# Two of each block's eight left-hand one-hots on GpSimd, in the gate stage of a hybrid Hyena/GLA/PEER layer

## What is computed

```python
best, pos = lax.top_k(cand_s, PEER_TOPK)
idx = jnp.take_along_axis(cand_i, pos, axis=-1)
gate = jax.nn.softmax(best, axis=-1)
...
a = jax.nn.gelu(jnp.einsum('td,tkd->tk', xt, u_tab[it]))
return jnp.einsum('tk,tkd->td', gt * a, v_tab[it])
```

## Time and profile before

| | |
|---|---|
| median of 3 runs | 2192.99 us (2191.74, 2192.99, 2200.29) |
| profiled execution, its own time | 2182.85 us |
| its span | 2181.1 us |
| TensorE busy | 2045.7 us, 94% of the span |
| VectorE busy | 1522.5 us, 70% |
| ScalarE busy | 822.2 us, 38% |
| GpSimd busy | 688.2 us, 32% |
| gate stage, first to last left-hand one-hot | 925.7 to 1403.5 us |
| granted TensorE clock, mean of the span | 0.97 of full speed |

### The profile page before, as it was taken

The page is one execution under the profiler, slowest core; times in us unless marked ns, Lnnn a source line. Parts: engine busy times, 40 slices in busy tenths (PEclk is TensorE's granted clock), DMA queues, the critical chain, the costliest instruction groups (busy, mean ns, idle before and its releaser), DMA issues.

```text
span 2181.1 us, 28455 instructions
## 1 busy us (share of the span) xinstructions
PE 2045.7 (94%) x9877; PEld 1631.1 (75%) x9877; DVE 1522.5 (70%) x3164; ACT 822.2 (38%) x1507; POOL 688.2 (32%) x469
## 2 busy tenths in 40 slices
PE   7999999797998999898888899979999999999998
PEld 3554454645998999887777788878888888888886
DVE  4221415623789999898888888748887687877876
ACT  2111004323212233477777778632222222222222
POOL 0000001003223665433333322224443255545551
PEclk7999999898999999999999999999999999999999
DMA  9121203415112465489999999989999899999994
GB/s 337 66 77 39 83 0 138 173 71 202 40 40 67 155 197 163 144 297 348 348 367 367 343 315 329 334 325 386 380 339 351 292 342 329 345 337 343 336 342 159
DMA packets 183919, 526.01 MB, mean 241 GB/s; under 512 B 16775, under 2 KB 67111, under 8 KB 181256
## 3 DMA queue, kind: packets, MB, share of 16 engines
q1 hardware_dynamic: 128520, 323.41, 40.9%
q0 software_dynamic: 55296, 201.35, 25.7%
HBM read 460.48 MB, written 64.23 MB: 241 GB/s over the span
## 4 chain that ended last, share of the span: by engine, by line
PE 64%; DVE 18%; DMA 9%; issue 5%; ACT 4%; SPq 0%; POOL 0%; ACTq 0%; DVEq 0%
PE ps L1014 32%; DMA ugat<-in_u_rows,idxs 7%; PE ps L664 5%; PE ps L947 4%; DVE junk L1478 3%; PE ps L883 3%; PE ps L757 3%; PE ps L919 3%; PE ps L920 3%; PE ps L723 3%; DVE oneh L1415 2%; PE ps L987 2%; ACT uhi L1738 2%; DVE eA L1496 2%; PE ps L663 1%
## 5 line engine op out<-in xcount | busy, mean ns | idle before, releaser
L947 PE MATMUL ps<-h2hi,uhi 128*128 128x384 f32 x1024 | 399.6, 390 | 32.7 <-issue 19.0
L1886 POOL DMA_INDIRECT ugat<-in_u_rows,idxs x256 | 268.5, 1049 | 512.2 <-DVE dots L1478 501.7
L1014 PE MATMUL ps<-vhi,whi 128*128 128x512 f32 x1024 | 399.1, 390 | 5.1 <-DVE wlo L1525 5.1
L1014 PE MATMUL ps<-vlo,whi 128*128 128x512 f32 x1024 | 399.1, 390 | 0.0
L1014 PE MATMUL ps<-vhi,wlo 128*128 128x512 f32 x1024 | 399.1, 390 | 0.0
L947 PE MATMUL ps<-h2lo,uhi 128*128 128x384 f32 x1024 | 351.3, 343 | 0.0
L947 PE MATMUL ps<-h2hi,ulo 128*128 128x384 f32 x1024 | 349.2, 341 | 0.0
L1816 ACT ACTIVATE vhi<-vraw 128x1024 fp32r<-128x1024 f32 x128 | 135.5, 1061 | 465.8 <-PE ps L1014 445.2
L1894 POOL DMA_INDIRECT vgat<-in_v_tab,idxs x128 | 214.7, 1677 | 222.9 <-DVE y L1536 179.2
L987 PE MATMUL ps<-eA,eB 128*128 128x128 f32 x1024 | 212.2, 289 | 51.9 <-DVE eA L1496 41.0
L987 PEld LDWEIGHTS ps<-eA,eB 128*128 128x128 f32 x1024 | 181.0, 193 | 91.9 <-DVE eA L1496 63.3
(11 more groups left out here) (275 smaller groups left out, 3064.2 us busy)
## 6 DMA issues: line engine op xcount, KB each, us to landing
uraw<-in_u_t SPq DMA_DIRECT2D x128, 512.0 KB, 5.6
vraw<-in_v_tab SPq DMA_DIRECT2D x128, 512.0 KB, 6.9
gate_scratch<-gst SPq DMA_DIRECT2D x16, 2048.0 KB, 13.1
gin<-gate_scratch SPq DMA_DIRECT2D x32, 1024.0 KB, 12.5
wring<-in_w_ada SPq DMA_DIRECT2D x12, 2048.0 KB, 9.4
gelu_scratch<-aout SPq DMA_DIRECT2D x128, 192.0 KB, 4.4
ain<-gelu_scratch SPq DMA_DIRECT2D x32, 768.0 KB, 7.8
wring<-in_w_in SPq DMA_DIRECT2D x6, 2048.0 KB, 8.6
```

The costliest lines, as they stand in the source:

```text
L947: last = pe.matmul(ps[:, b % 4, 0:TA], w[:, b % 2, k, :], h[:, k, LP:LP + TA], start=(k == 0 and j == 0), stop=(k == KD - 1 and j == 2))
L1014: last = pe.matmul(ps[:, y_bank(t) + h, :], w[:, b, (t - 1) * P:t * P], v[:, b, h * 512:(h + 1) * 512], start=(start and j == 0), stop=(st ...
L1886: pool.indirect_dma_start(out=ugat[:, g % GSLOT], out_offset=None, in_=u_rows, in_offset=bass.IndirectOffsetOnAxis(ap=idxs[:, g // HK, g % ...
```

## The change

Of each four tokens the third (`q % 4 == 2`, so k = 2 and k = 6 of each block) has its eA made by GpSimd, with the same operation and into the same ring slot, and counts on a semaphore of its own, `onehot_p_ready`. VectorE skips these two. TensorE waits for each one-hot on the semaphore of the engine that made it. GpSimd now goes through the stage block by block: it waits for `cl_drained` once (the indices are in `cols_hk`), and in each block it makes the two one-hots, each after the wait for its ring slot, and then issues the gathers that follow that block's dots. The gathers beyond the stage go on as before.

```diff
+def pool_row(q):
+    return q % 4 == 2
+
+
+def rows_before(q, on_pool):
+    return sum(pool_row(i) == on_pool for i in range(q))
...
+        onehot_p_ready = sem("onehot_p_ready")
...
-                        pe.wait_ge(onehot_ready, tok + 1)
+                        ready = onehot_p_ready if pool_row(q) else onehot_ready
+                        pe.wait_ge(ready, it * rows_before(P, pool_row(q)) + rows_before(q + 1, pool_row(q)))
...
-                    if q >= RING:
-                        dve.wait_ge(onehot_used, q + 1 - RING)
-                    dve.tensor_scalar(eA[:, q % RING], iota[:], cols_hk[:, 0, q:q + 1], cols_hk[:, 2, q:q + 1],
-                                      ALU.is_equal, ALU.mult).then_inc(onehot_ready, 1)
+                    if not pool_row(q):
+                        if q >= RING:
+                            dve.wait_ge(onehot_used, q + 1 - RING)
+                        dve.tensor_scalar(eA[:, q % RING], iota[:], cols_hk[:, 0, q:q + 1], cols_hk[:, 2, q:q + 1],
+                                          ALU.is_equal, ALU.mult).then_inc(onehot_ready, 1)
...
             pool.wait_ge(idx_ready, 2)
-            for g in range(GSLOT, NDOT):
+            pool.wait_ge(cl_drained, NTD)
+            for n in range(BLK_A, BLK_C):
+                if n == BLK_A + TURN_U + 1:
+                    pool.wait_ge(w_taken, 1)
+                for q in range(TB * (n - BLK_A), TB * (n - BLK_A + 1)):
+                    if pool_row(q):
+                        if q >= RING:
+                            pool.wait_ge(onehot_used, q + 1 - RING)
+                        pool.tensor_scalar(eA[:, q % RING], iota[:], cols_hk[:, 0, q:q + 1], cols_hk[:, 2, q:q + 1],
+                                           ALU.is_equal, ALU.mult).then_inc(onehot_p_ready, 1)
+                for g in dots_at(n):
+                    gather_u(g + GSLOT)
+            for g in range(dots_before(BLK_C) + GSLOT, NDOT):
                 gather_u(g)
```

## The result

| | before | after |
|---|---|---|
| median of 12 runs | 2191.70 us (2189.31 to 2201.86) | 2197.89 us (2192.49 to 2202.89) |
| ratio, 95% interval | | 1.0030 (1.0019 to 1.0041) |
| profiled execution | 2182.85 us | 2202.89 us |
| GpSimd busy | 688.2 us, 32% | 874.7 us, 40% |
| VectorE busy | 1522.5 us, 70% | 1501.5 us, 68% |

The kernel became 6.2 us slower by the medians; the interval excludes 1 and lies within 0.5%. Of the 20 us, 4.1 lie ahead of the stage's first low part (927.87 us before, 931.94 after), where nothing was changed.

What follows compares the result with a forecast made beforehand. Quiet blocks were held bound by a 6.91 us chain across TensorE, ScalarE and VectorE, bursts by full DMA engines. Terms 0 + 0 + 0 + 2 gave 2185 us profiled, 2195 against the median; range 2182 to 2220.

Steps and rivals of the forecast that it cites:

- the chain: Quiet gate-stage block: ScalarE's split, VectorE's low part, eA of k=4, its dot, eA of k=5, TensorE's k=5; 6.91 us round.
- "Worth 0" for the relief: VectorE in quiet blocks: dropping two of eight eA frees 0.52 us, idle ahead of the low part, gaining 0.
- The price of a one-hot: GpSimd's compare-and-scale of 128 columns: 0.46 us, range 0.2 to 1.27, from its products and subtractions.
- rival A: Quiet three-dot blocks, slower: above 0.49 us a one-hot, GpSimd's pair holds off VectorE's low part; 2211 to 2235 us, chance 0.25.
- The term of the bursts: Around 2 MB stores: the gather after the dot of k=1 goes 0.4 us later, at six long waits; 2 us.
- the sum: All terms over the gate stage: 0 + 0 + 0 + 2 = 2 us slower.
- Rival B: Bursts, faster: a late dot of k=1 no longer keeps back TensorE's k=2; 5 to 9 us off, about 2186, chance 0.10.

## Why the prediction was right, and which terms were off

**The chain held.** The quiet period was to stay at 6.91 to 6.92 us, in blocks with three dots and with two, and did. (VectorE's wait before the low part was to be about 0.8 us; the forecast's own terms, 0.16 + 0.52, give 0.68, and it is 0.56.) That k=2 and k=6 are off the chain and k=4 and k=5 on it was shown from both sides: taking the first two away gives 0, and taking the other two away gives 6.92 to 5.97 where GpSimd has room. "Worth 0" for the relief is right taken alone; the run with the one-hots made twice points to what the sentence leaves out, that GpSimd used the freed time.

**The price of a one-hot was too low.** The forecast took 0.46 us, inside 0.2 to 1.27. Measured: 0.80 at the least, 1.18 in the mean. This is beyond the 0.49 from which rival A decides: at 0.8 it gave 2211 us.

**Rival A didn't come, by luck of the timing.** The pair runs into the low part in each quiet block, as A had it, and the low part starts on time all the same. The forecast read from the earlier trace rows that either engine holds the other for its whole instruction. GpSimd is indeed held by VectorE: the first one-hot of the quiet block takes 1.09 us, to 1104.74, as 0.80 from about the end of the dot of k=1 would. VectorE is held by GpSimd too, but for less than the 0.80 us that the profile records for a one-hot. A low part that came 0.13 us into a one-hot took 1.56 us instead of 1.22; one that comes 0.28 us into it, as in the quiet block, takes its usual 1.23. The Trainium skill (SBUF — State Buffer, section SBUF: two separate sides) says that whichever starts first gets the shared port for the whole instruction. By that rule the low part would have been over 1.22 us after 1105.54, at 1106.76; in this trace it is over at 1106.25, and the measurement decides. So two errors met, a price too low and a hold too strong, and the room between them is small: had the low part come 0.15 us earlier in each of A's 26 quiet blocks, 26 x 0.34 = 9 us would be an estimate of the loss.

**The term of the bursts was too small.** The forecast took 6 x 0.4 = 2 us for a gather 0.4 late. In the quiet block the gather starts 1.35 us late, and is stretched by 0.51 as it falls into the low part, 1.86 in all. Measured: 6.2 us for the whole change against the 2 of the sum. The run with the waits alone, where a gather is 1.5 us late and GpSimd has no one-hot, has 3.7 us (0.2 to 7). How the 6.2 divide between late gathers and blocks bound by GpSimd stays open.

**A sentence that failed.** The forecast would be wrong "if TensorE waited for GpSimd's k=2, which needs one-hots over 0.9 us". TensorE did, in 16 places, and one-hots are over 0.9 us in the mean; the time stayed in the range all the same, because these blocks are few, and only in bursts and behind them. The sum counted each engine's place in one block, but never GpSimd's fill: 6.0 of 6.92 us in a quiet block, 6.6 at the means of the stage, 8.27 in a block behind a burst. That leaves little room for a neighbour of this change: made twice, spread, with k=4 and k=5, or with VectorE packed closer, it loses 16 to 41 us against the kernel before.

Rival B (faster in the bursts) has nothing for it: the waits for late gathers grew in every kernel with the pair in its three-dot blocks.

## What to carry to other kernels

Before moving an operation to an idle-looking engine, follow the chain round one block and see whether the operation is on it; a block with less of the same work is a ready test. Then count what the receiving engine has to do in one period, at durations that hold beside the work of its neighbour, together with the DMA issues queued behind. Here the gains lay in the order of one engine's work and in the size of the stores, which took 50 us off together.

## What the runs showed of the hardware

- A 128x128 compare-and-scale takes GpSimd 0.80 us when it starts outside VectorE's two-input instructions, and VectorE makes one each 0.26 us. The Trainium skill (GPSIMD Engine Reference, section Engine selection) calls one-input work on GpSimd roughly line-rate; at this size the trace has it slower than VectorE by a factor of three.
- The issue of a gather of 128 rows takes GpSimd 0.94 to 1.03 us, and from there up to 2.08 when it starts inside a VectorE instruction with two inputs of 128x1024. One that starts just before a dot and runs beside most of it still takes 0.94 (1102.67, dot at 1102.85). In the kernel with the waits alone 0.94 and 1.93 us stand in the same block, for the same instruction.
- GpSimd can hold VectorE too: a dot or low part that starts 0.13 us into a one-hot takes 1.56 us instead of 1.22, one that starts 0.28 us in takes 1.23.
- On GpSimd, a semaphore instruction of its own ahead of a gather, its wait met, came with a start 0.72 us behind it, in 62 of 64 blocks; no run separates the cause.
- The granted clock is 1.00 over the first 45 blocks once the stores are spread, and was 0.96 before: in a burst, where TensorE waits for the late dots, it read 0.87 and, after the change, 0.81. TensorE's clock has the levels 2.4 and 1.2 GHz; these are means of the two.
